# State-space diagonal product with its operands swapped: the result comes out transposed, two heads side by side in column groups, and the other terms of y are added by identity products

## The reference, cut to what matters

```python
seg = acs[:, :, :, None] - acs[:, :, None, :]
lmat = jnp.exp(jnp.where(lower, seg, -jnp.inf))
cb = jnp.einsum('bcign,bcjgn->bcijg', cc, bc)
wmat = cb[..., None] * lmat * dtc[:, :, None]
y_diag = jnp.einsum('bcijgr,bcjgrp->bcigrp', wmat, xc)
...
y_off = jnp.einsum('bcign,bcgrpn->bcigrp', cc, starts) * jnp.exp(acs)[..., None]
y = (y_diag + y_off).reshape(b, n, SSD_HEADS, SSD_HEADDIM)
...
y = y_f + jnp.flip(y_b, 1) + xs.astype(jnp.float32) * d_skip.astype(jnp.float32)[:, None]
y = y.reshape(b, n, SSD_DI) * jax.nn.silu(z.astype(jnp.float32))
y = rmsnorm(y, norm_g).astype(h.dtype)
return y @ w_out, s_f, s_b
```

## Time and profile before

| | |
|---|---|
| runs before, median of 3 | 2079.45 us (2075.62 to 2081.21) |
| the profiled execution, its own time | 2075.3 us |
| its span in the profile | 2073.5 us |
| TensorE busy, matmul | 1937.1 us, 93% |
| TensorE busy, weight load | 1820.1 us, 88% |
| VectorE busy | 1067.8 us, 51% |
| ScalarE busy | 605.7 us, 29% |
| GpSimd busy | 1197.1 us, 58% |
| mean granted clock of TensorE | 0.962 |

### The profile page before, as it was taken

One profiled execution on the slowest core, in us unless ns is written; L12 is line 12 of the kernel. 1 busy time (PEld: TensorE's weight loads), 2 busy tenths in 40 slices (PEclk: granted clock), 3 DMA queues, 4 the chain that ended last, 5 costly groups with the idle time before them and its releaser, 6 DMA issues. The chain is left out here.

```text
span 2073.5 us, 33494 instructions
## 1 busy us (share of the span) xinstructions
PE 1937.1 (93%) x12945; PEld 1820.1 (88%) x12945; DVE 1067.8 (51%) x1700; ACT 605.7 (29%) x1152; POOL 1197.1 (58%) x869
## 2 busy tenths in 40 slices
PE   5999887999999999988999999987899999999997
PEld 3878776989999999988998989976799999999997
DVE  4466672455325524637366666668425641661453
ACT  3244320122102201214454656565212210220121
POOL 2433333566676677774554555532487777777764
PEclk7899987999999999998999999988999999999999
DMA  9311109556436322231333332311422222222212
GB/s 288 120 35 45 40 24 308 178 155 183 132 102 183 111 63 81 59 114 52 105 112 102 101 114 92 113 61 52 125 78 62 79 63 80 72 71 72 71 56 76
DMA packets 293063, 208.82 MB, mean 101 GB/s; under 512 B 7480, under 2 KB 285021, under 8 KB 292445
## 3 DMA queue, kind: packets, MB, share of 16 engines
q1 hardware_dynamic: 292957, 207.32, 32.9%
HBM read 196.63 MB, written 10.67 MB: 100 GB/s over the span
## 5 line engine op out<-in xcount | busy, mean ns | idle before, releaser
L891 POOL TENSOR_SCALAR w_hi<-raw 128x512 fp32r<-128x512 f32 (+1 forms) x432 | 646.7, 1514 | 851.8 <-PE ps L925 776.3
L895 POOL TENSOR_TENSOR w_lo<-raw,w_hi 128x512 fp32r<-128x512 f32 (+1 forms) x432 | 557.3, 1311 | 0.0
L925 PE MATMUL ps<-h_hi,w_hi 128*128 128x322 f32 (+1 forms) x1688 | 414.4, 327 | 5.9 <-DVE h_lo L2120 3.3
L925 PE MATMUL ps<-h_lo,w_hi 128*128 128x322 f32 (+1 forms) x1688 | 389.8, 312 | 0.0
L925 PE MATMUL ps<-h_hi,w_lo 128*128 128x322 f32 (+1 forms) x1688 | 389.0, 312 | 0.0
L925 PEld LDWEIGHTS ps<-h_hi,w_hi 128*128 128x128 f32 x1688 | 286.0, 192 | 25.9 <-issue 22.6
L925 PEld LDWEIGHTS ps<-h_hi,w_lo 128*128 128x128 f32 x1688 | 287.3, 190 | 0.0
L925 PEld LDWEIGHTS ps<-h_lo,w_hi 128*128 128x128 f32 x1688 | 285.9, 190 | 0.0
L925 PE MATMUL ps<-g_hi,w_hi 128*128 128x322 f32 (+1 forms) x816 | 192.8, 318 | 11.6 <-DVE g_lo L2079 11.4
L925 PE MATMUL ps<-g_lo,w_hi 128*128 128x322 f32 (+1 forms) x816 | 190.8, 316 | 0.0
L925 PE MATMUL ps<-g_hi,w_lo 128*128 128x322 f32 (+1 forms) x816 | 190.2, 315 | 0.0
(11 more groups left out here) (326 smaller groups left out, 2973.1 us busy)
## 6 DMA issues: line engine op xcount, KB each, us to landing
ada<-in_ada_w SPq DMA_DIRECT2D x48, 1024.0 KB, 6.3
raw<-in_ffn_w_up SPq DMA_DIRECT2D x88, 512.0 KB, 3.9
raw<-in_ssd_w_in SPq DMA_DIRECT2D x40, 512.0 KB, 4.1
R<-scr_acs SPq DMA_DIRECT2D x40, 512.0 KB, 4.7
raw<-in_ffn_w_down SPq DMA_DIRECT2D x32, 512.0 KB, 4.2
raw<-in_att_w_in SPq DMA_DIRECT2D x16, 512.0 KB, 6.1
raw<-in_ssd_w_out SPq DMA_DIRECT2D x16, 512.0 KB, 4.1
raw<-in_ffn_w_down SPq DMA_DIRECT2D x16, 384.0 KB, 3.5
```

The costliest lines, as they stand in the source:

```text
L891: nc.gpsimd.tensor_scalar(w_hi[j % 2][:, a_:b_, :], raw[j][:, a_:b_, :], 1.0, None, ALU.mult).then_inc(w_hi_done, 1)
L895: ins = nc.gpsimd.tensor_tensor(w_lo[j % 2][:, a_:b_, :], raw[j][:, a_:b_, :], w_hi[j % 2][:, a_:b_, :].bitcast(F32), ALU.subtract)
L925: ins = mm(out[:, cols], w[slot][:, k, :], x[:, cols], start=first and k == 0 and i == 0, stop=last and k == n - 1 and i == 2)
```

## The change

`yd` swaps its operands. The stationary operand is now the 64 columns of xdt of one head, and the moving one the 128 columns of R. The result is y transposed, [64 channels, 128 tokens]. The even heads write PSUM partitions 0 to 63 and the odd heads 64 to 127, in column groups of the array, so that the bank holds what `yT` made before. What else belongs to y (x times d_skip, and `yo` for chunks 1 to 4) is gathered in y1 and then added to the same bank by four products with y1 as the stationary operand and the identity as the moving one. The event `yT` and its transposes go, and so does the addition of the bank on VectorE; the product with silu(z) moves to `yd`. `yo` moves ahead of `yd` in the table, to the half tile before `cb` of its own chunk. The fetch of R waits on `R_used` for both directions, which the last product of each direction counts.

```diff
--- before.py
+++ after.py
@@ -173,10 +173,9 @@
             put(*slots[at], "cb", g, c)
             if c < 4:
                 put(*slots[at], "csf", g, c)
+            if c:
+                put(*slots[at - 1], "yo", g, c)
             put(*slots[at + 2], "yd", g, c)
-            if c:
-                put(*slots[at + 3], "yo", g, c)
-            put(*slots[at + 6], "yT", g, c)
         put(*slots[10], "stT", g)
         if g == GROUPS - 1:
 
...
@@ -797,10 +796,8 @@
 
 
                 g, c = divmod(n, CHUNKS)
-                if n and d_ == 0:
-                    sp.wait_ge(R_used, n)
-                elif n:
-                    sp.wait_ge(ssd_mm, SSD_USE[("yd", (n - 1) // CHUNKS, (n - 1) % CHUNKS)] + 1)
+                if n:
+                    sp.wait_ge(R_used, 2 * n - 1 + d_)
                 src = scr_acs[c, 32 * d_ + g * GH:32 * d_ + (g + 1) * GH, :]
                 sp.dma_start(R[:, d_, :, :], src.partition_broadcast(P)).then_inc(R_in[d_], 16)
 
...
@@ -1312,9 +1309,15 @@
                     for d_ in range(2):
                         pe.wait_ge(W_done, 2 * (CHUNKS * g + ev[2]) + d_ + 1)
                         for r in range(GH):
-                            ins = mm(bank(b, HD, r * HD), R[:, d_, r, :], xdt[:, d_, r * HD:(r + 1) * HD],
-                                     start=(d_, r) == (0, 0), stop=(d_, r) == (1, GH - 1), skip_group_check=True)
-                        ins.then_inc((R_used, ssd_mm)[d_], 1)
+                            half = HD * (r % 2)
+                            ins = mm(bank(b, P, (r // 2) * P)[half:half + HD, :], xdt[:, d_, r * HD:(r + 1) * HD],
+                                     R[:, d_, r, :], start=d_ == 0 and r < 2, stop=False, skip_group_check=True)
+                        ins.then_inc(R_used, 1)
+                    pe.wait_ge(y_done, 5 * g + ev[2] + 1)
+                    for q_ in range(4):
+                        ins = mm(bank(b, P, q_ * P), y1[ev[2] % 2][:, q_ * P:(q_ + 1) * P], ident, start=False,
+                                 stop=q_ == 3, skip_group_check=True)
+                    ins.then_inc(ssd_mm, 1)
                 elif kind == "yo":
                     c = ev[2]
 
@@ -1325,12 +1328,6 @@
                         b = ssd_begin(ev + (d_,))
                         src = st_f[c % 2][:, :] if d_ == 0 else st_b[:, c - 1, :]
                         mm(bank(b), cT[g % 2][:, cols], src, start=True, stop=True).then_inc(ssd_mm, 1)
-                elif kind == "yT":
-                    pe.wait_ge(y_done, 5 * g + ev[2] + 1)
-                    b = ssd_begin(ev)
-                    for q_ in range(4):
-                        ins = tr(bank(b, P, q_ * P), y1[ev[2] % 2][:, q_ * P:(q_ + 1) * P], ident)
-                    ins.then_inc(ssd_mm, 1)
                 elif kind == "stT":
                     pe.wait_ge(st_done, CS_AT[("csf", g, 0)] + 1)
                     for d_ in range(2):
...
@@ -2192,6 +2189,15 @@
                     dve.wait_ge(ssd_mm, SSD_USE[CS_LIST[i - 2]] + 1)
                 tt(h64(xw[i % 2][:, :]), h64(x_tok[g % 2][:, c, :]), per_head(wst, c, 0 if kind == "csf" else 1, g),
                    ALU.mult).then_inc(xw_done, 1)
+
+            def skip_term(g, c):
+
+                if c >= 2:
+                    dve.wait_ge(ssd_mm, SSD_USE[("yd", g, c - 2)] + 1)
+                elif g:
+                    dve.wait_ge(ssd_mm, SSD_USE[("yd", g - 1, 4)] + 1)
+                return tt(h64(y1[c % 2][:, :]), h64(x_tok[g % 2][:, c, :]), bc(d_bc[:, GH * g:GH * (g + 1)], 2, HD),
+                          ALU.mult)
 
             n_id = 0
             for ev in SSD:
@@ -2274,8 +2280,10 @@
                     if n:
                         dve.wait_ge(W_done, 2 * n)
                     tt(cbm[:, :, :], bc(bank(b, P), 1, 2), masks, ALU.mult).then_inc(ssd_free_dve, 1)
+                    if c == 0:
+                        skip_term(g, 0).then_inc(y_done, 1)
                     if n:
-                        dve.wait_ge(ssd_mm, SSD_USE[("yd", g, c - 1) if c else ("yd", g - 1, 4)] + 1)
+                        dve.wait_ge(R_used, 2 * n)
                     else:
                         dve.wait_ge(acs_stored, 16)
                     for d_ in range(2):
@@ -2286,21 +2294,14 @@
                         dve.wait_ge(seg_exp, 2 * n + d_ + 1)
                         tt(R[:, d_, :, :], R[:, d_, :, :], bc(cbm[:, d_, :], 1, GH), ALU.mult).then_inc(W_done, 1)
                 elif kind == "yd":
-                    n = 5 * g + c
-                    y_ = y1[c % 2][:, :]
-
-                    if c >= 2:
-                        dve.wait_ge(ssd_mm, SSD_USE[("yT", g, c - 2)] + 1)
-                    elif g:
-                        dve.wait_ge(ssd_mm, SSD_USE[("yT", g - 1, 4)] + 1)
-                    chain(tt(h64(y_), h64(xt), bc(d_bc[:, GH * g:GH * (g + 1)], 2, HD), ALU.mult))
                     b = ssd_wait(ev)
-                    tt(y_, y_, bank(b), ALU.add).then_inc(ssd_free_dve, 1)
-                    dve.wait_ge(*ssd_end(ev))
                     if c == 0:
-                        nc.vector.memset(small[:, 60:61], 0.0).then_inc(y_done, 1)
+                        dve.wait_ge(acc_free_act, acc_ends[A_E + 10 * g + 9][1])
+                    dst = yg[:, 4 * g:4 * g + 4, chunk_col(c):chunk_col(c) + P]
+                    tt(dst, bank(b).rearrange("p (q n) -> p q n", q=4), dst, ALU.mult).then_inc(ssd_free_dve, 1)
                 elif kind == "yo":
                     y_ = y1[c % 2][:, :]
+                    chain(skip_term(g, c))
                     for d_ in range(2):
                         b = ssd_wait(ev + (d_,))
                         tt(h64(y2[:, :]), h64(bank(b)), per_head(eacs, c, d_, g), ALU.mult).then_inc(ssd_free_dve, 1)
@@ -2311,12 +2312,6 @@
                         else:
                             ins.then_inc(y_done, 1)
                             dve.wait_ge(y_done, 5 * g + c + 1)
-                elif kind == "yT":
-                    b = ssd_wait(ev)
-                    if c == 0:
-                        dve.wait_ge(acc_free_act, acc_ends[A_E + 10 * g + 9][1])
-                    dst = yg[:, 4 * g:4 * g + 4, chunk_col(c):chunk_col(c) + P]
-                    tt(dst, bank(b).rearrange("p (q n) -> p q n", q=4), dst, ALU.mult).then_inc(ssd_free_dve, 1)
 
 
             for k in range(12, 16):
```

More of the change, by code:

```diff
@@ L199 @@
 SSD_READER = {"dtT": "dve", "sum": "dve", "acsT": "act", "trB": "act", "trx": "act", "init": "act", "csb": "dve", "csf": "dve", "cb": "dve", "yd": "dve",
-              "yo": "dve", "yT": "dve", "stT": "act"}
+              "yo": "dve", "stT": "act"}
 SSD_USE, SSD_END = uses_of(
@@ L856, in _ @@
                 beside(tile)
-            sp.wait_ge(*ssd_end(("yT", 3, 4)))
+            sp.wait_ge(*ssd_end(("yd", 3, 4)))
             sp.wait_ge(st_stored, 128)
@@ L1612, in y_high @@
                     act.wait_ge(mm_done, T_E + 40)
-                act.wait_ge(*ssd_end(("yT", k // 4, 4)))
+                act.wait_ge(*ssd_end(("yd", k // 4, 4)))
                 A_(y_hi[:, k, :], yg[:, k, :], ACT.Copy, scale=pcol("ssd_norm_g", k)).then_inc(yn_hi, 1)
@@ L1635, in _ @@
                     if i < 2 and g >= 2:
-                        act.wait_ge(y_done, 5 * (g - 1))
+                        act.wait_ge(*ssd_end(("yd", g - 2, 4)))
                     if i == 2 and g:
```

## The result

The changed kernel takes 2058.1 us (median of 4 runs, 2057.47 to 2058.76), the kernel before 2079.6 on the same chip: a ratio of 0.9911, 95% interval 0.9892 to 0.9931. It is faster. The profiled execution has a span of 2055.9 us, 17.6 less than the one before, where the sum said 24.7.

What follows compares the result with a forecast made beforehand. The prediction took TensorE, busy 93% of the span, to bound the kernel, with chains of waits in the rest of group 3. Terms of 10.7, 6.3, 0.9 and 6.8 gave 24.7 us less, hence 2053 us, range 2040 to 2068.

Steps and rivals of the forecast that it cites:

- the sum: Whole kernel: gains of 10.7, 6.3, 0.9 and 6.8 us make 24.7 us less; its case got 0.70, 2040 to 2061.
- The price of the swap: Each chunk on TensorE: yd 1.93 us plus identity products 0.87, so 2.80 us in place of 3.92.
- the lost bank wait: Groups 0 to 2: the B transposes no longer wait for the bank that yT held, 2.7 us gained.
- both waits of chunk 3: Before yd of chunk 3, groups 0 to 2: TensorE waits for R, 1.1 us and 2.4 us for the two directions.
- the stages of group 3: Group 3: 6.3 us less to row 7, 0.9 from there to yd of chunk 4, 6.8 from there to row 12.
- about 0.3 us in chunk 0: Chunk 0 of groups 0 to 2: a wait for R's second product, three times, 1 us back.
- the first rival: Groups 0 to 2: R's chain holds every chunk, leaving about 2062 to 2066 us; chance 0.14.
- 7.8 us given back: Chunk 3 of groups 0 to 2: waits for R grow from 0.9 to 3.5 us, in three groups 7.8 us lost.
- Taking turns: In yd the array's halves do not run side by side: yd costs 3.7 us, 2074 to 2082 in all; chance 0.07.
- loads in the open: In yd weight loads can't run beside products: 5.2 us in place of 3.49, near 2108 us in all; chance 0.09.

Runs made afterwards that it cites:

- evens_first: The changed kernel with the eight heads of a yd in the order 0, 2, 4, 6, 1, 3, 5, 7: 2062.0 us, ratio 0.992.
- yo_early_2: The kernel before with yo ahead of its yd and yT behind yd of two chunks later, operands, transposes and addition as before: 2082.4 us, ratio 1.0025.
- fill: The changed kernel with 14 products of constants in front of yd of chunk 3 in groups 0 to 2: 2050.9 us, ratio 0.988.
- tail_fill: The changed kernel with chunk 3's yd later and R's loads kept in place (groups 0-2), plus 25 constant products before yd of group 3, chunk 1: 2052.8 us.

## Why the prediction was right, and where a step of it failed

The 2053 us were 5 below the median, inside the range; the case that came is that of the sum, near its upper end. The price of the swap, the lost bank wait, both waits of chunk 3 and the stages of group 3 came as written. One term of the sum was mis-sized.

*The products.* Right. `yd` takes 1.9 us for 1.93 and the identity products 0.9 to 1.0 for 0.87. The records of `yd` start in pairs 7 ns apart, and a pair follows a pair at 0.109. The rule of the Trainium skill, "TensorE: Matmul & The Clock Gate", section "Part 3: Packing small matmuls", that a load overlaps a product only in another row group, does not hold here: 32 loads on all rows take 1.73 us within the products' 1.97. (The same section also lets a load into a background weight buffer go ahead; no row here can tell whether that is what happens.) The section "Back-to-back issue gap" of that page has loads and products go through a reorder window. But the page moves only loads in it: "Part 3" has products start and end in the order of the program. As the trace of evens_first records the starts, the other half begins ahead of three records that stand before it, so here the measurement differs, and it decides.

*The bank wait, 2.7 us.* Right: the row is gone. yo_early_2, which moves `yo` but keeps `yT`, keeps it too (2.5 us), so the new place of `yo` is not what removes it. That `yT`'s bank is, follows from the rotation.

*Chunks 0 and 3.* The waits were right: about 0.3 us in chunk 0, 1.1 and 2.15 in chunk 3 for 1.1 and 2.4. No other chunk of groups 0 to 2 waits for R, so the first rival did not come.

*The failed step* is the price of chunk 3's waits, "7.8 us given back": it counted the time waited and nothing for the work behind it. The forecast named the low clock only as the upper edge of the case, and for the first rival. The trace shows 17.0 us of low clock there. Groups 0 to 2 fall short of their sum by 10.7 - 3.5 = 7.2 us. Of these 5.4 are the low clock: fill, whose products stand in the time of the waits, and evens_first, whose waits are shorter, show no low clock there and give the same figure. Another 1.2 is the wait of `yo` of chunk 4 for the state, which the sum did not have either; it shows in fill and is hidden behind the low clock in the changed kernel (an estimate from 3 x 0.4). Then 0.6 is left for all other terms. With both, the sum is 24.7 - 6.6 = 18.1 us, and the stretches that the change touches gave 3.5 + 7.5 + 7.2 = 18.2. The 1.5 us ahead of them and the 2.1 behind, which make it 17.6, are no part of the change.

*Group 3.* Right, stage by stage. From the first `yd` to `cb` of chunk 4 (1417.07) it is 6.6 us less for the 6.3 of the sum, from there to `yd` of chunk 4 0.85 for 0.9, and from that to row 12 (1443.87) 6.7 for 6.8. From row 12 to the products behind the norm another 0.5 went, which the sum did not have. The rows of the y product there still wait twice for GpSimd's w_lo, 6.1 and 5.3 us, which the sum had left in place.

*The other rivals.* Taking turns and loads in the open both fall with the 1.9 us.

Open: behind 1459.62 it took 2.1 us more, with 26.3 us of low clock for the 20.8 of before. By the traces of the other kernels the two go together. Why the low clock is granted for 15, 21 or 26 us in one and the same code was not tried.

## What to carry to other kernels

With half-width stationary operands in two column groups, 32 records of 128 moving columns took 1.90 us, where by the pace of one group they would take 3.5 (an estimate, 32 x 0.109). The two groups need not alternate strictly, but order has a price: four in a row made it 2.50. When a saving makes TensorE arrive early at a chain of other engines, price the wait and also the work behind it at half clock; then either give TensorE something to do there, or move the waiting step behind work that is ready, and check on every queue what moves with it. Here two loads of R, 512 KB each, behind a weight load on SyncE decided between 2062 and 2049 us. And before a median is believed, compare the stretches that the edit does not touch: here they differed by up to 5 us behind the norm.

## What the runs showed of the hardware that was not expected

- Two waits of 1.1 and 2.15 us, 1.1 us of products between them, brought the low clock; 1.1 and 1.7 us, with 1.5 us between them, did not (evens_first). Yet 1.1 and 1.3 us, with 2.0 us between them, did (yo_early_2). So the length of the waits alone does not tell, and what does is open.
- Useless products instead of a wait made groups 0 to 2 5.4 us shorter (fill). Where the next wait followed soon they only moved the low clock, and their stretch became 2.5 us longer (tail_fill).
- One and the same code behind the norm took 591.6 us with 14.8 us of low clock and 596.2 to 596.6 with 26.2 to 26.6.
- With the heads in the order 0, 2, 4, 6, 1, 3, 5, 7, the other column half started ahead of three records that stand before it in the program (evens_first).
